# Hand-ordered queues of a two-model forward pass: SSD slots, a gated-conv branch and the opening in another order

## The chip, the cores and the metric

The kernel runs on one core of a Trainium2 chip. The metric is device time in microseconds (us), lower is better. Before the change it is 1112.82 us, the median of 3 runs (1112.5 to 1112.93).

## What is computed

Two models in a row on 256 tokens of width 1024 (272 with 16 meta tokens in the first). The first has an SSD (state space) mixer, a squared-ReLU MLP, a latent-attention mixer and another MLP; the second has a block with neighbourhood attention and a short gated convolution side by side, and an MLP. Cut to the parts that the change touches:

```python
# SSD mixer (8 groups of 4 heads, state 128, chunk 128)
z, xbc, dt = split(h @ w_in)
xbc = silu(causal_depthwise_conv(xbc, conv_w, conv_b))        # width 4
xs, b_in, c_in = split(xbc)
dt = softplus(dt + dt_bias);  a = -exp(a_log)
a_cs = cumsum(dt * a)
y = sum over s <= l of (C_l . B_s) * exp(a_cs[l] - a_cs[s]) * dt_s * x_s   # + d_skip * xs
g = y * silu(z);  g = g * rsqrt(mean(g * g, group) + eps) * norm_g;  out = g @ w_out

# second model's block
q, k, v, cb, cc, ch, ga, gb = split(rms_norm(x) @ w_in)
y_a = neighbourhood_attention(q, k, v, rpb) @ w_attn_branch
y_b = (cb * conv3(cc * ch)) @ w_conv_branch
x = x + (sigmoid(ga) * y_a + sigmoid(gb) * y_b) @ w_o
```

## The kernel before

Activations lie with features on the 128 partitions and tokens in the free dimension. Every fp32 product is made of three fp32r matmuls: weight and input are each split in a rounded part (`w_hi`, `x_hi`) and the rest (`w_lo`, `x_lo`), and PE adds hi*hi, hi*lo and lo*hi (`tile`, L450 ff). Weights stream as pages of 128x1024: SP loads a page into one of four slots `w_raw`, ACT rounds it (`hi`, L942), DVE or POOL subtracts (`lo`, L1423 on DVE, L2060 on POOL), PE uses it. A pair of pages is a chunk; `lin_chunk(c, k, n)` (L467) first waits until the PSUM buffer of its parity has been drained (`free`), then runs the two pages into `lin`.

There is no scheduler. Each engine's program is written out by hand, and the order of its lines is the order of its queue; semaphores join the queues.

**Opening** (L491 ff on PE, L974 ff on ACT, L1459 ff on DVE). The first norm's squares are summed by eight matmuls on ones; two of the squares are made on DVE (`square_raw`), six on ACT (`square_h` and L992). Meanwhile dt and the first group's x are projected from the unnormalised input. DVE scales dt, adds the bias (L1489), makes its modulus (L1491, L1493), ACT takes exp and ln of it, and DVE makes softplus, the product with a and the running sum `acs` (L1497 to L1502), before it drains the first x (`first_xs`, L1508). POOL writes `acs` to DRAM and reads it back, broadcast over the partitions (`acs_rows`), for the decays that ACT makes (`decay_logs`, `decay`).

**SSD slots** (`slot` on each engine). Slot s makes three projections for group s (x; B and C; z), the scan of group g = s-1, and the group norm of gs = s-2. PE: first projection, `cb_products`, `x_transposes`, second projection, `group_stat` (ones times `y_sum`), third projection, `y_products`. ACT: two decays, the z sigmoid (exp, ln, exp), page c+2.0, `conv0` (the convolution's first tap), page c+2.1, the square of y2, decay logs, the x sigmoid, and so on. DVE: `w_lo` of page c+2.0, `causal_cb`, the three other taps (`conv`, L1533), the clamp before the sigmoid, `scaled_tokens`, `head_mix`. POOL: the acs rows, y2, y_sum, then the `w_lo` of three pages. Slots 0 and 1 are written out, 2 to 7 in loops, 8 and 9 without projections.

**Second block** (`for i in range(20)` on PE, ACT and DVE). Iteration i projects chunk i, which DVE drains. Beside it runs the attention: head n has its maxima, exp and weighting (`weigh2`) in iteration n+6 of ACT and DVE; PE transposes its probabilities into ps7 at the top of iteration n+8 (L890), and DVE copies ps7 to `p_t2` in its iteration n+7, behind its second page. `values2(j)` (L901) multiplies heads 2j and 2j+1, behind the projection in PE's iteration 2j+9. `yb` = cb * conv is made on DVE at the end of iterations 10 and 11, rounded on ACT (`yb_hi`), and its rest `yb_lo` follows at once on DVE.

```python
    pe.wait_ge(pt2_done, 2 * j + 2)            # values2(j)
```

## Time and profile before

| | before |
|---|---|
| median of 3 runs | 1112.82 us |
| profiled execution, its own time | 1112.04 us |
| its span | 1110.4 us |
| granted PE clock | 1.00 of full speed |
| PE, weight loads busy | 1096.2 us (99%), 1067.3 us (96%) |
| DVE, ACT, POOL busy | 766.8 us (69%), 653.5 us (59%), 165.0 us (15%) |
| DMA | 171 GB/s mean |

The span runs from the first to the last instruction. A busy PE is one that has a matmul in flight; an idle stretch is named after the instruction that ended it. DVE is VectorE, ACT is ScalarE, POOL is GpSimd. In the slots DVE and ACT are busy for over nine tenths of the time, elsewhere for about half.

### The profile page before, as it was taken

What the parts mean: (1) busy time and instruction counts of PE and PEld (TensorE: products, weight loads), DVE (VectorE), ACT (ScalarE), POOL (GpSimd) and SP (SyncE); (2) the same over time, 40 slices, a digit from 0 to 9 for tenths busy, and PEclk for the clock granted to TensorE, in tenths of its full rate; (3) what the DMA queues carried; (4) which work ended last, traced back from release to release, by engine and by line L of the source; (5) the groups of instructions that cost most, each with busy time, mean ns of one, the idle gap of its engine ahead of it and who ended that gap; (6) DMA issues with size and microseconds to landing.
All of it is one profiled execution on the core that took longest, in us unless ns stands there. A gap on an engine that the chain in (4) does not pass through costs nothing.

```text
span 1110.4 us, 24004 instructions
## 1 busy us (share of the span) xinstructions
PE 1096.2 (99%) x8963; PEld 1067.3 (96%) x8963; DVE 766.8 (69%) x1154; ACT 653.5 (59%) x1075; POOL 165.0 (15%) x152
## 2 busy tenths in 40 slices
PE   9999999999999999999999999999999999999998
PEld 8999999999999999988899999999998999999998
DVE  7988999778565555588686665558787687666543
ACT  7899999655554433577565554446546655555331
POOL 0435434317000000112020000000003201000000
PEclk9999999999999999999999999999999999999999
DMA  6544544585545454443265555555444555555552
GB/s 240 205 157 156 185 153 159 151 260 167 174 171 179 163 187 171 134 136 113 73 213 188 182 187 181 181 195 172 152 151 144 182 181 187 183 189 188 182 182 91
DMA packets 53226, 189.96 MB, mean 171 GB/s; under 512 B 5920, under 2 KB 7200, under 8 KB 53168
## 3 DMA queue, kind: packets, MB, share of 16 engines
q1 hardware_dynamic: 51408, 182.59, 48.5%
...
q8 instruction: 38, 0.62, 0.2%
...
HBM read 188.07 MB, written 1.08 MB: 170 GB/s over the span
## 4 chain that ended last, share of the span: by engine, by line
PE 70%; DVE 14%; ACT 9%; issue 4%; DMA 2%; ACTq 0%; POOL 0%; DVEq 0%; SPq 0%
PE lin L462 22%; PE lin L464 22%; PE lin L463 22%; DVE w_lo L1426 4%; ACT w_hi L947 3%; DMA w_raw<-w 2%; DVE cv L1533 1%; ACT cv L1038 1%; ACT ee L1062 1%; DVE sg L1543 1%; ACT sg L1021 1%; ACT dd L1052 1%; DVE s_m L1836 1%; ACT sg L1019 1%; ACT pr L1347 1%
## 5 line engine op out<-in xcount | busy, mean ns | idle before, releaser
L1426 DVE TENSOR_TENSOR w_lo<-w_raw,w_hi 128x1024 fp32r<-128x1024 f32 (+3 forms) x318 | 382.2, 1204 | 252.6 <-ACT w_hi L947 251.9
L947 ACT ACTIVATE w_hi<-w_raw 128x1024 fp32r<-128x1024 f32 (+2 forms) x342 | 351.9, 1034 | 225.6 <-PE lin L464 212.9
L462 PE MATMUL lin<-x_hi,w_hi 128*128 128x256 f32 (+1 forms) x1504 | 432.3, 287 | 3.0 <-DVE cv L1533 2.4
L464 PE MATMUL lin<-x_hi,w_lo 128*128 128x256 f32 (+1 forms) x1504 | 428.4, 285 | 0.0
L463 PE MATMUL lin<-x_lo,w_hi 128*128 128x256 f32 (+1 forms) x1504 | 427.4, 284 | 0.0
L462 PEld LDWEIGHTS lin<-x_hi,w_hi 128*128 128x128 f32 x1504 | 283.6, 189 | 5.9 <-issue 3.6
L464 PEld LDWEIGHTS lin<-x_hi,w_lo 128*128 128x128 f32 x1504 | 283.8, 189 | 0.0
L463 PEld LDWEIGHTS lin<-x_lo,w_hi 128*128 128x128 f32 x1504 | 283.0, 188 | 0.5
L464 PE MATMUL lin<-hid_hi,w_lo 128*128 128x256 f32 (+1 forms) x768 | 218.2, 284 | 0.0
L463 PE MATMUL lin<-hid_lo,w_hi 128*128 128x256 f32 (+1 forms) x768 | 217.9, 284 | 0.0
L462 PE MATMUL lin<-hid_hi,w_hi 128*128 128x256 f32 (+1 forms) x768 | 217.4, 283 | 0.0
L464 PEld LDWEIGHTS lin<-hid_hi,w_lo 128*128 128x128 f32 x768 | 145.1, 189 | 0.0
L462 PEld LDWEIGHTS lin<-hid_hi,w_hi 128*128 128x128 f32 x768 | 145.0, 189 | 0.0
L463 PEld LDWEIGHTS lin<-hid_lo,w_hi 128*128 128x128 f32 x768 | 144.3, 188 | 0.0
L2058 POOL TENSOR_TENSOR h_sq<-h_sq 128x256 f32<-128x256 f32 (+1 forms) x35 | 30.3, 865 | 448.5 <-ACT h_sq L960 447.1
L1167 ACT ACTIVATE relu<-lin 128x512 f32<-128x512 f32 (+1 forms) x48 | 29.1, 606 | 82.6 <-PE lin L464 82.6
L2063 POOL TENSOR_TENSOR w_lo<-w_raw,w_hi 128x1024 fp32r<-128x1024 f32 x24 | 58.7, 2447 | 74.2 <-ACT w_hi L947 74.2
L956 ACT ACTIVATE x_hi<-h,vecs 128x256 fp32r<-128x256 f32 (+2 forms) x40 | 20.3, 508 | 42.1 <-DVE h L1708 37.7
L462 PE MATMUL lin<-g_hi,w_hi 128*128 128x272 f32 x144 | 42.2, 293 | 0.8 <-issue 0.4
L1691 DVE TENSOR_TENSOR hid_lo<-relu_sq,hid_hi 128x512 f32 (+1 forms) x48 | 34.4, 717 | 11.2 <-DVE relu_sq L1687 11.2
L464 PE MATMUL lin<-g_hi,w_lo 128*128 128x272 f32 x144 | 41.7, 289 | 0.0
L463 PE MATMUL lin<-g_lo,w_hi 128*128 128x272 f32 x144 | 41.5, 288 | 0.0
...
## 6 DMA issues: line engine op xcount, KB each, us to landing
...
```

What stands on the lines that cost most here:

```text
L462: mm3(o, wh, xh, start=first and i == 0, stop=False)
L463: mm3(o, wh, xl, start=False, stop=False)
L464: ins = mm3(o, wl, xh, start=False, stop=last and i == kts - 1)
L947: a(w_hi[pg.slot][:, 0:n], w_raw[pg.slot][:, 0:n], ACT.Copy).then_inc(w_hi_done, pages)
L956: a(x_hi[:, kt.value, 0:width(norm)], h[:, kt.value, tokens(norm)], ACT.Copy, scale=gain(norm, kt.value)).then_inc(xh_done, 1)
L1019: a(buf, buf if x is None else x, ACT.Exp, scale=-1.0).then_inc(step_sem, 1)
L1021: a(buf, buf, ACT.Ln, bias=1.0).then_inc(step_sem, 1)
L1167: a(relu[i][:, :, 0:n], linp(k, slice(0, n)), ACT.Relu).then_inc(drained[k.parity], 1)
L1426: tt(w_lo[pg.slot][:, 0:n], w_raw[pg.slot][:, 0:n], w_hi[pg.slot][:, 0:n].bitcast(F32), ALU.subtract)\
L1691: tt(hid_lo[:, bass.ds(at.value, 2), 0:n], relu_sq[i][:, :, 0:n], hid_hi[:, bass.ds(at.value, 2), 0:n].bitcast(F32), ALU.subtract).then_in ...
L2058: tt(h_sq[:, 0, 0:n], h_sq[:, 0, 0:n], h_sq[:, kt, 0:n], ALU.add).then_inc(hsum_done, 1)
L2063: tt(w_lo[pg.slot][:, 0:n], w_raw[pg.slot][:, 0:n], w_hi[pg.slot][:, 0:n].bitcast(F32), ALU.subtract)\
```

## The change

It adds and removes no matmul and no page. What moves:

- Opening: squares 6 and 7 go from ACT to DVE, before its last two `raw_lo`. The dt bias and the modulus are done by ACT (Abs and Relu with a bias) instead of three DVE instructions, and the three sums of dt come on DVE after `first_xs` and another page. On POOL two `w_lo` stand ahead of the wait for the acs write.
- Slots: on ACT `conv0` and both pages stand ahead of the z sigmoid; on DVE `w_lo` of page c+2.0 comes after the convolution; on POOL the first `w_lo` comes before y_sum, and the acs rows for the next slot are fetched before the last `w_lo` of this one; on PE the group statistic moves into the middle of the third projection.
- Second block: the copy to `p_t2` moves from behind the second page of DVE's iteration n+7 to the top of n+8; `yb` from the end of 10 and 11 to the top of 11 and 12; `yb_hi` and `yb_lo` to 11 and 12.

```diff
@@ -493,7 +493,7 @@
             for kt, (squared, count) in enumerate(((hsq_done, 1), (hsq_done, 2), (hsq_dve, 1), (hsq_dve, 2),
-                                                   (hsq_done, 3), (hsq_done, 4), (hsq_done, 5), (hsq_done, 8))):
+                                                   (hsq_done, 3), (hsq_done, 8), (hsq_dve, 3), (hsq_dve, 4))):
@@ -510,7 +510,7 @@
-                pe.wait_ge(dt_dve, 5)
+                pe.wait_ge(dt_dve, 3)
@@ -577,10 +577,11 @@
                 if has_lin:
                     lin_chunk(c + 1, k + 1, T, 0 if first else None)
-                if has_stat:
-                    group_stat(s + (-2))
-                if has_lin:
-                    lin_chunk(c + 2, k + 2, T)
+                    free(k + 2)
+                    for j in range(2):
+                        tile(lin[:, 2 * (k + 2).parity + j, 0:T], (c + 2).page(j), x_hi, x_lo, T).then_inc(w_used, 1)
+                        if has_stat and j == 0:
+                            group_stat(s + (-2))
@@ -984,12 +985,10 @@
             square_h(0, At(4))
-            square_h(0, At(5))
+            a(h_sq[:, 5, :], h[:, 5, :], ACT.Square).then_inc(hsq_done, 5)
             round_raw(6)
             round_raw(7)
             hi(Page(0), DT_PAGE, pages=2)
-            square_h(0, At(6))
-            a(h_sq[:, 7, :], h[:, 7, :], ACT.Square).then_inc(hsq_done, 3)
             hi(Page(2))
             norm_inv(0)
             hi(Page(3))
@@ -1002,10 +1001,14 @@
             hi(At(2).page(0))
+            dt_bias = v(V_DTB, rows=slice(0, 32))
+            act.wait_ge(drained[0], 1)
+            a(dta[:, :], dtb[:, :], ACT.Abs, bias=dt_bias).then_inc(dt_act, 1)
             round_hn(4)
-            act.wait_ge(dt_dve, 2)
+            act.wait_ge(dt_act, 2)
             a(dta[:, :], dta[:, :], ACT.Exp, scale=-1.0).then_inc(dt_act, 1)
-            act.wait_ge(dt_act, 2)
+            a(dtx[:, :], dtb[:, :], ACT.Relu, bias=dt_bias).then_inc(dt_act, 1)
+            act.wait_ge(dt_act, 3)
             a(dta[:, :], dta[:, :], ACT.Ln, bias=1.0).then_inc(dt_act, 1)
             round_hn(5)
@@ -1067,13 +1070,14 @@
                     decay(g, 0)
                     decay(g, 1)
+                if has_lin:
+                    conv0(s, 0)
+                    hi((c + 2).page(0))
+                    hi((c + 2).page(1))
+                if has_scan:
                     kz = g.times(3, K_GRP + 2)
                     act.wait_ge(drained[kz.parity], kz.half + 1)
                     sigmoid(z_sg[:, :, :], zg_step, g.times(3), z_raw[:, :, :])
-                if has_lin:
-                    hi((c + 2).page(0))
-                    conv0(s, 0)
-                    hi((c + 2).page(1))
                 if has_stat:
                     act.wait_ge(y2_done, (gs + 1).value)
                     a(h_sq[:, 0:2, :], y2[:, :, :], ACT.Square).then_inc(ysq_done, 1)
@@ -1392,8 +1396,8 @@
                     exps2(i - 6)
-                if i in (10, 11):
-                    j = i - 10
+                if i in (11, 12):
+                    j = i - 11
                     act.wait_ge(yb_done, j + 1)
                     a(yb_hi[:, 2 * j:2 * j + 2, :], yb[:, 2 * j:2 * j + 2, :], ACT.Copy).then_inc(ybh_done, 1)
@@ -1467,8 +1471,12 @@
-            for kt in range(2, KD):
+            for kt in range(2, 6):
                 raw_lo(kt)
+            square_raw(6)
+            square_raw(7)
+            raw_lo(6)
+            raw_lo(7)
             lo(Page(0), DT_PAGE)
             dve.sem_inc(w_lo_done[1], 1)
             lo(Page(2))
@@ -1484,30 +1492,22 @@
                 if kt == 1:
                     dve.wait_ge(w_used, 1)
                     tt(dtb[:, :], lin[r32, 0, 0:T], r_inv[r32, :], ALU.mult).then_inc(drained[0], 1)
-                if kt == 2:
-                    dve.wait_ge(drained[0], 1)
-                    ts(dtb[:, :], dtb[:, :], v(V_DTB, rows=r32), None, ALU.add).then_inc(first_bias, 1)
...
-                    tt(dta[:, :], dtb[:, :], dtx[:, :], ALU.max).then_inc(dt_dve, 1)
                 if kt in (3, 5):
                     lo(At(2).page(kt // 2 - 1))
-            dve.wait_ge(dt_act, 3)
-            stt(dt_t[:, :], dtb[:, :], 0.0, dta[:, :], ALU.max, ALU.add).then_inc(dt_dve, 1)
...
-            nc.vector.tensor_tensor_scan(acs[:, :], cst[r32, N_ONES:N_ONES + 1].broadcast_to([32, T]), dtx[:, :],
             lo(At(3).page(0))
...
             lo(At(3).page(1))
+            dve.wait_ge(dt_act, 5)
+            tt(dt_t[:, :], dtx[:, :], dta[:, :], ALU.add).then_inc(dt_dve, 1)
+            dve.wait_ge(dt_dve, 1)
+            ts(dtx[:, :], dt_t[:, :], a_exp[:, 0:1], -1.0, ALU.mult, ALU.mult).then_inc(dt_dve, 1)
...
+            nc.vector.tensor_tensor_scan(acs[:, :], cst[r32, N_ONES:N_ONES + 1].broadcast_to([32, T]), dtx[:, :],
@@ -1616,10 +1616,10 @@
                 if has_lin:
-                    lo((c + 2).page(0))
                     if has_scan:
                         causal_cb(g)
                     conv(s, 0)
+                    lo((c + 2).page(0))
                     clamp(sg[:, 0:2, :], cv[:, 0:2, :]).then_inc(clamped, 1)
@@ -1934,6 +1934,17 @@
             for i in range(20):
                 c, k = At(C_IN2 + i), At(K_IN2 + i)
+                if 8 <= i < 16:
+                    dve.wait_ge(pT2_done, i - 7)
...
+                    nc.vector.tensor_copy(p_t2[i % 2][:, :], ps7[:, :]).then_inc(pt2_done, 1)
+                if i in (11, 12):
+                    j = i - 11
+                    dve.wait_ge(drained[(k + (-1)).parity], (k + (-1)).half + 1)
...
+                    tt(yb[:, 2 * j:2 * j + 2, :], cv2[:, 2 * j:2 * j + 2, :], cb_r[:, 2 * j:2 * j + 2, :], ALU.mult)\
+                        .then_inc(yb_done, 1)
                 lo((c + 2).page(0))
                 dve.wait_ge(w_used, (c + 1).page().value)
@@ -1950,11 +1961,6 @@
                 lo((c + 2).page(1))
-                if 7 <= i < 15:
-                    dve.wait_ge(pT2_done, i - 6)
...
-                    nc.vector.tensor_copy(p_t2[(i + 1) % 2][:, :], ps7[:, :]).then_inc(pt2_done, 1)
@@ -1999,12 +2005,8 @@
                 if 6 <= i < 14:
                     weigh2(i - 6)
-                if i in (10, 11):
-                    j = i - 10
...
-                    tt(yb[:, 2 * j:2 * j + 2, :], cv2[:, 2 * j:2 * j + 2, :], cb_r[:, 2 * j:2 * j + 2, :], ALU.mult)\
-                        .then_inc(yb_done, 1)
+                if i in (11, 12):
+                    j = i - 11
                     dve.wait_ge(ybh_done, j + 1)
@@ -2070,10 +2072,8 @@
-            def slot(s, has_lin=True, has_stat=True):
+            def slot(s, has_lin=True, has_stat=True, has_rows=True):
                 c, gs = s.times(3, C_GRP), s + (-2)
-                if has_lin and s.base:
-                    acs_rows(s)
                 if has_stat:
...
                     tt(y2[:, :, :], y1[:, :, :], z_s[gs.parity][:, :, :], ALU.mult).then_inc(y2_done, 1)
+                if has_lin:
+                    lo((c + 2).page(1))
+                if has_stat:
                     pool.wait_ge(ysq_done, (gs + 1).value)
                     tt(y_sum[:, :], h_sq[:, 0, :], h_sq[:, 1, :], ALU.add).then_inc(ysum_done, 1)
                 if has_lin:
-
-                    lo((c + 2).page(1))
                     lo((c + 3).page(1))
+                    if has_rows:
+                        acs_rows(s + 1)
                     lo((c + 4).page(1))
 
-            pool.wait_ge(dt_dve, 5)
+            pool.wait_ge(dt_dve, 3)
             pool.dma_start(acs_dram, acs[:, :]).then_inc(acs_out, 16)
+            lo(At(C_GRP + 3).page(0))
+            lo(At(C_GRP + 3).page(1))
             pool.wait_ge(acs_out, 16)
             acs_rows(At(0))
-            lo(At(C_GRP + 3).page(0))
-            lo(At(C_GRP + 3).page(1))
             lo(At(C_GRP + 4).page(1))
+            acs_rows(At(1))
             slot(At(1), has_stat=False)
             with pool.Fori(0, 2) as turn:
                 for i in range(2):
                     slot(At(2 + i, 2, turn))
             slot(At(6))
-            slot(At(7))
+            slot(At(7), has_rows=False)
             slot(At(8), has_lin=False)
             slot(At(9), has_lin=False)
```

How the queues stand. First ACT in the loop over the SSD slots, just after the two decays (ee): before,

```order
L1062 ACTIVATE ee<-dd 128x864
L1071 ISA
L1019 ACTIVATE z_sg<-z_raw 128x544
L1020 ISA
L1021 ACTIVATE z_sg<-z_sg 128x544
L1022 REGISTER_ALU
L1023 ACTIVATE z_sg<-z_sg 128x544
L944 ISA
L946 ISA
L947 ACTIVATE w_hi<-w_raw 128x1024
L1032 REGISTER_ALU
```

and in the change (cv is conv0):

```order
L1065 ACTIVATE ee<-dd 128x864
L1035 ISA
L1041 ISA
L1041 REGISTER_ALU
L1041 ACTIVATE cv<-lin,vecs 128x272
L1041 ISA
L1041 ACTIVATE cv<-lin,vecs 128x272
L945 ISA
L947 REGISTER_ALU
L948 ACTIVATE w_hi<-w_raw 128x1024 x2
L1079 REGISTER_ALU
L1022 ACTIVATE z_sg<-z_raw 128x544
```

The two instructions of conv0 and the two pages now stand between the decays and the z sigmoid. Second, POOL in the same loop, one turn of the change:

```order
L2083 TENSOR_TENSOR y<-y,z_s 128x544
L2064 ISA
L2065 TENSOR_TENSOR w_lo<-w_raw,w_hi 128x1024
L2088 TENSOR_TENSOR y_sum<-h_sq 128x272
L2064 REGISTER_ALU
L2065 TENSOR_TENSOR w_lo<-w_raw,w_hi 128x1024
L2071 REGISTER_ALU
L2073 ISA
L2073 DMA acs_bc<-acs_dram 128x1088
L2064 REGISTER_ALU
L2065 TENSOR_TENSOR w_lo<-w_raw,w_hi 128x1024
```

Before, the DMA stood ahead of the product y2 (written y here), y_sum right behind it, and the three w_lo in a row at the end. Third, DVE from the weighting of head 4 (pr) to the next maxima in the second block: before,

```order
L1932 TENSOR_SCALAR pr<-pr,rinv 128x256 x2
L2006 TENSOR_TENSOR cv<-cv,cb_r 128x512
L2010 TENSOR_TENSOR yb_lo<-cv,yb_hi 128x512
L1426 TENSOR_TENSOR w_lo<-w_raw,w_hi 128x1024
L1951 TENSOR_TENSOR cb_r<-lin,r_inv 128x512
L1426 TENSOR_TENSOR w_lo<-w_raw,w_hi 128x1024
L1957 COPY p_t<-ps 128x512
L1987 TENSOR_TENSOR ya_lo<-ps,ya_hi 128x256
```

and in the change:

```order
L1932 TENSOR_SCALAR pr<-pr,rinv 128x256 x2
L1941 COPY p_t<-ps 128x512
L1946 TENSOR_TENSOR cv<-cv,cb_r 128x512
L1430 TENSOR_TENSOR w_lo<-w_raw,w_hi 128x1024
L1962 TENSOR_TENSOR cb_r<-lin,r_inv 128x512
L1430 TENSOR_TENSOR w_lo<-w_raw,w_hi 128x1024
L1993 TENSOR_TENSOR ya_lo<-ps,ya_hi 128x256
```

cv<-cv,cb_r is yb. Its rest, yb_lo, no longer follows it but comes behind the next weighting; the copy of ps7 has changed places with a page, a drain and a page.

## Rows read from the trace of the kernel before

**Rows 1.** What TensorE (PE) waited for, whole span: waiting line <- releaser: total us, times, longest.
```profile
PE ps L890 <- DVE pr L1932: 2.9, 3, 1.3
PE lin L462 <- DVE cv L1533: 2.4, 5, 0.8
...
PE ps L540 <- DVE bc_s L1547: 0.4, 1, 0.4
...
PE lin L462 <- issue: 0.4, 1, 0.4
PE ps L548 <- POOL y_sum L2085: 0.3, 1, 0.3
...
PE lin L462 <- DVE g_lo L1577: 0.3, 1, 0.3
```
**Rows 2.** Timeline of PE in SSD slots: start us, duration us, instruction, count [idle before].
```profile
55.52 0.24 PE L567 MATMUL ps<-mm,x_tok 128*64 128x16 f32 x4
55.69 0.39 PE L462 MATMUL lin<-x_hi,w_hi 128*128 128x272 f32 x1
...
130.42 0.62 PE L540 MATMUL ps<-bc_s 128*128 128x272 f32 x2
...
138.12 0.62 PE L548 MATMUL ps<-y_sum,cst 128*128 128x272 f32 x2
...
146.30 0.24 PE L567 MATMUL ps<-mm,x_tok 128*64 128x16 f32 x4
146.93 0.39 PE L462 MATMUL lin<-x_hi,w_hi 128*128 128x272 f32 x1 [0.39 <-DVE cv L1533]
```
**Rows 3.** Timeline of ScalarE (ACT) in the same slot.
```profile
130.76 0.64 ACT L1019 ACTIVATE z_sg<-z_raw 128x544 f32<-128x544 f32 x1
...
132.69 1.04 ACT L947 ACTIVATE w_hi<-w_raw 128x1024 fp32r<-128x1024 f32 x1
...
136.74 1.95 ACT L1052 ACTIVATE dd<-acs_bc,cols 128x272 f32<-128x272 f32 x6 [0.58 <-DMA acs_bc<-acs_dram]
139.69 0.66 ACT L1019 ACTIVATE sg<-sg 128x544 f32<-128x544 f32 x1 [1.00 <-DVE sg L1543]
```
**Rows 4.** Timeline of VectorE (DVE) in the same slot.
```profile
133.76 1.23 DVE L1426 TENSOR_TENSOR w_lo<-w_raw,w_hi 128x1024 fp32r<-128x1024 f32 x1 [1.67 <-ACT w_hi L947]
...
138.03 1.63 DVE L1543 TENSOR_SCALAR sg<-cv 128x544 f32<-128x544 f32 x1
...
144.28 2.51 DVE L1533 SCALAR_TENSOR_TENSOR cv<-lin,vecs,cv 128x271 f32<-128x271 f32 x6
146.90 0.45 DVE L1543 TENSOR_SCALAR sg<-cv 128x544 f32<-128x544 f32 x1
```
**Rows 5.** Timeline of GpSimd (POOL) in the same slot.
```profile
136.97 2.38 POOL L2063 TENSOR_TENSOR w_lo<-w_raw,w_hi 128x1024 fp32r<-128x1024 f32 x1
144.65 2.37 POOL L2063 TENSOR_TENSOR w_lo<-w_raw,w_hi 128x1024 fp32r<-128x1024 f32 x1 [5.29 <-ACT w_hi L947]
```
**Rows 6.** Timeline of PE in the opening, second projection.
```profile
22.08 0.29 PE L464 MATMUL lin<-x_hi,w_lo 128*128 128x272 f32 x1
22.49 0.39 PE L462 MATMUL lin<-x_hi,w_hi 128*128 128x272 f32 x1
```
**Rows 7.** Timeline of PE, then of DVE, in the second block's attention.
```profile
833.52 0.66 PE L890 MATMUL ps<-cst,pr 128*128 128x128 f32 x4 [1.08 <-DVE pr L1932]
...
839.80 1.08 PE L901 MATMUL ps<-p_t,v 128*64 128x256 f32 x8
842.20 0.66 PE L890 MATMUL ps<-cst,pr 128*128 128x128 f32 x4 [1.32 <-DVE pr L1932]
...
825.76 0.69 DVE L2010 TENSOR_TENSOR yb_lo<-cv,yb_hi 128x512 fp32r<-128x512 f32 x1 [0.70 <-ACT yb_hi L1398]
826.71 1.23 DVE L1426 TENSOR_TENSOR w_lo<-w_raw,w_hi 128x1024 fp32r<-128x1024 f32 x1 [0.26 <-ACT w_hi L947]
...
835.72 1.23 DVE L1426 TENSOR_TENSOR w_lo<-w_raw,w_hi 128x1024 fp32r<-128x1024 f32 x1 [0.26 <-ACT w_hi L947]
```

20 lines of the change are left out of this document (7 added, 13 removed).

## The prediction

> **What bounds the kernel now.** I read the page first: TensorE (PE) is busy in 99% of the span, at the full granted clock, and the other engines are well below it. So the time is the sum of the PE's matmuls plus the moments in which it waits, and an edit that adds or removes no matmul can only move those moments. The second view is the list of what PE waited for [rows 1]. All of it is small: the longest groups are 2.9 us before the transposes of the probabilities (L890) and 2.4 us before projections behind the convolution on VectorE (DVE, L1533). The third view is the timeline of each engine in one SSD slot [rows 2 to 5], the fourth the opening [rows 6], the fifth the second block's attention [rows 7]. Everything outside them (the MLPs, the MLA block) is untouched.
>
> **The SSD slots.** A slot on PE is: first projection, cb products and x transposes, second projection, group statistic, third projection, y products. After the last y matmul the next slot's projection starts 0.63 us later (146.30 to 146.93), where the trace also shows the same step without a wait: 0.17 us (55.52 to 55.69) [rows 2]. So a stalled slot loses 0.46 us, of which 0.39 is shown as idle. Rows 1 have five such waits with 2.4 us and one put down to issue with 0.4; with 0.07 of refill for each of the six that makes 3.2 us. That is the most the slots can give.
>
> Why is the convolution late? I follow it back. The slot's second convolution starts on DVE at 144.28, right behind work that runs without a gap from 133.76. There DVE had stood idle for 1.67 us until ScalarE (ACT) rounded the page w_hi [rows 4]. ACT came to that page at 132.69, because the z sigmoid (three instructions from 130.76, 1.93 us) stood ahead of it [rows 3]. In the same chain the clamp at 138.03 takes 1.63 us where its like at 146.90 takes 0.45: it lies under POOL's w_lo (from 136.97, 2.38 us long) and ends 0.3 us after it [rows 4, 5]. ACT then waits 1.00 us for that clamp, and before it 0.58 us for the DMA of acs rows [rows 3].
>
> The change puts conv0 and both w_hi pages ahead of the z sigmoid, takes w_lo page 0 behind the convolution on DVE, lets POOL do its w_lo before y_sum, and issues the acs DMA a slot part earlier. I count from E, the end of the first projection (130.42). Before, conv0 ran at E+3.2. Now ACT is free at E+0.3 (130.76), so conv0 ends at E+1.3, and the two pages at E+2.2 and E+3.2 (a page row is 1.04 long [rows 3], about 1 us each). POOL's w_lo follows: E+3.2 to E+5.6 (2.4). DVE has the cb products at about E+1.0, masks them (0.6), convolves (2.5) and is at w_lo page 0 at E+4.1; POOL holds it off until E+5.6, so it ends at E+6.8. The z sigmoid and the square (1.93+0.6) end on ACT at E+5.8; y_sum (0.8) then stands behind that w_lo, and the clamp behind y_sum: clamp done near E+8.0, against 139.66 = E+9.2 before. ACT and DVE gain about 1.2 us, more than the 0.46 that is missing. After six slots without the stall the chain still has about 0.8 us to spare, so I take the whole 3.2 us. Bounds: 0 (the chain finds another brake) and 3.2.
>
> Here the lock matters. In this trace an op of DVE that reads two SBUF tiles or clamps one ends 0.3 us behind POOL's w_lo, while the convolution, which reads PSUM and one SBUF tile, takes 2.51 us under POOL's w_lo of 144.65 as well [rows 4, 5]. The Trainium skill, SBUF — State Buffer, section Who interferes with whom, states it as an exclusive lock for whole instructions between GpSimd and DVE ops with two SBUF inputs or in a two-port mode; the rows agree with it. Without a lock page 0 would be ready at E+5.3 instead of E+6.8. PE wants it at 138.12 = E+7.7 [rows 2]: either way in time, so the sum stays, but by the lock only 0.9 us is left, and on that the slower rival below rests.
>
> The group statistic moves behind the third projection's first page. It costs what it costs now; PE does the same matmuls. Its cover only grows: y_sum is due 3 us later.
>
> **Behind the last slot** PE waits once for y_sum (0.3 us) and once for g_lo (0.3 us) [rows 1]. POOL and ACT come to y_sum 0.8 us earlier, so I take the first, with 0.2 of refill: 0.5 us. The g_lo chain hangs on the statistic itself; I take nothing for it, and 0.4 as the upper bound.
>
> **The opening.** Two squares leave ACT and are done by DVE before its last two raw_lo. ACT's next page is bound by its DMA there, so r_inv comes when it did; nothing gained, nothing lost. Three instructions on dt leave DVE's chain ahead of the w_lo and x_lo that PE waits for, and the dt sums go behind first_xs. PE's gap of 0.41 from 22.08 to 22.49, against a pace of 0.125, is such a wait: 0.28 us [rows 6]. The wait before the first cb products (0.4 in rows 1, 0.1 of refill) shrinks, since ACT gets to its sigmoids earlier. Together 0.8 us. What is made later: acs, by some 2 us, and the first acs rows behind two w_lo on POOL (2.4 each) [rows 5]. They are read on ACT some 10 us later, so I count nothing; if that cover is gone, ACT waits and the 0.8 is lost. Abs on ACT is not in this trace; the nearest row is the first step of the z sigmoid, 0.64 us on 128x544 [rows 3], and dt has 32x272, so with Relu it is 0 to 1.3 us of ACT time, of which most stands where ACT waited for DVE's modulus. I take nothing for it. The Trainium skill, ScalarE: Activation LUTs, section Table sets: the hidden batching unit, has abs and relu in every set, so by it no table is loaded for them; no row here shows Abs.
>
> **The second block.** PE waits for weigh2 (pr, L1932) three times, 2.9 us [rows 1]: 1.08 before 833.52, 1.32 before 842.20, just after the values of 839.80 [rows 7], and so 0.5 once more. DVE is late because iterations 10 and 11 carry yb: after yb it waits 0.70 us for ACT's yb_hi, and 0.26 us for the page behind that [rows 7]. In the change yb stands at the top of the next iteration and yb_lo at its end; ACT makes yb_hi while DVE scales pr, so both waits go: 0.96 us in each of two iterations, 1.9 us. And yb starts one iteration later, so the first late iteration is on time.
>
> But the copy of ps7 into p_t moves from the middle of an iteration to the top of the next, and PE's values2 need it. It has the shape of yb_lo, 0.69 us [rows 7]. Before, iteration 11 begins at 826.71 and 12 at 835.72 [rows 7], 9.0 us. In the change iteration 10 lacks yb, yb_lo and the waits (2 x 0.6 + 0.96), and since iteration 7 has no copy DVE comes about 0.8 us earlier all along: 11 begins at 823.7. It lasts 9.0-0.96 = 8.05, 12 (without the 0.35 of ya_lo) 7.7: iteration 13 begins at 839.4 and its copy ends at 840.0. PE, without its first wait, would be at these values at 839.80-1.08 = 838.7: a new wait of about 1.3 us. PE then starts the next transposes at 841.1, not 842.2, and the last wait (0.5, 0.2 of refill) is gone: gain 1.1+0.7 = 1.8 us. Bounds: 0, and 3.2 (2.9 and refill).
>
> **Sum.** 3.2+0.5+0.8+1.8 = 6.3 us. The profiled execution took 1112.04 us (span 1110.4 and 1.6 around it), so it would be 1105.7; the median of the runs, 1112.82, is 0.8 above it: **1106.5 us**.
>
> **Rivals.**
> - The second block gives nothing: values2 wait for the copy as long as the transposes did for pr. For it: the copy is due just as PE comes at every odd iteration. Against: DVE is freed of 1.9 us of waiting. 1108.3 us, chance 0.15.
> - The slots give half: ACT has only 1.58 us of idle time in a slot (0.58+1.00) and the slot shrinks by 0.46, so a new wait there leaves part of the stall. 1108.1 us, chance 0.12; with the one above, 1109.9.
> - Everything goes, the 3.2 of the second block and g_lo's wait too: 8.1 us, 1104.7 us, chance 0.05.
> - Slower: the third projection waits for w_lo page 0, in all six slots. It is ready at E+6.8, due at E+7.7; should ACT's second page, and POOL's w_lo and DVE's behind it, come over 0.9 us later than I count, each further microsecond costs six. At 2.4 us late it is 6 x 1.5 = 9 us: 1106.5+9 = 1115.5. It turns slower from 2.3 us late on. Against it: conv0 is tied to PE's own pace, and ACT has its idle time to catch up. Chance 0.05.
> - The change does not do what it says, since DVE and ACT drift to the same order of waits: 1112.8 us, chance 0.03.
>
> **Chances.** Forecast 0.60, rivals as above. A measurement of this kernel can tell about 0.2% (2.2 us) from no change, so faster means below 1110.6: the forecast and the first three rivals, 0.92, less 0.04 for mixtures that end near the bound: 0.88. Same 0.07, slower 0.05. The range: the low end is the full gain, 1104.5; the high end takes in most of the first two rivals together, 1109.6.
>
> **What would show it.** In the slots: no PE idle before the first projection; ACT's conv0 right behind decay; the DVE w_lo of page 0 longer than 1.2 us, ending 0.3 to 1.5 us behind POOL's; no idle before the dd rows; period of a slot near 22.2 us instead of 22.65. In the second block: one wait of PE before values2 near 840, of 1 to 1.5 us, and none for pr. In the opening: the gap near 22.3 gone, acs written about 2 us later. Wrong it is if PE shows waits for w_lo at the third projection, for acs DMA through ACT, or for p_t copies at each odd iteration.

## The result, and the profile after

The changed kernel takes 1104.33 us (median of 4 runs, 1103.82 to 1104.87) against 1112.66 us before in the same session: ratio 0.9925, 95% interval 0.9908 to 0.9942. That is 8.3 us less, where 6.3 were forecast, and 0.17 us below the low end of the range. Both profiled executions agree with it: 1112.04 us before, 1103.82 after (span 1102.1, clock 1.00), 8.2 less.

Medians of one kernel differ by 0.3 us between sessions (1112.66 to 1112.94 for the kernel before), so the parts are read from landmarks in PE's timeline. In kernels that share the code in question, the slots repeat within 0.3 us (150.29 to 150.55) and the second block within 0.1 (58.84 to 58.92). First what PE waits for after the change, the answer to [rows 1] (waiting line <- releaser: total us, times, longest):

```profile
PE ps L494 <- DVE mm L1447: 1.3, 1, 1.3
PE ps L902 <- DVE p_t L1941: 0.7, 1, 0.7
PE lin L737 <- POOL q_n L2160: 0.5, 1, 0.5
PE lin L462 <- DVE x_lo L1440: 0.4, 2, 0.2
PE ps L768 <- DVE o_lo L1858: 0.4, 1, 0.4
PE lin L505 <- DVE w_lo L1430: 0.3, 1, 0.3
PE ps L784 <- DVE p_t L1854: 0.3, 1, 0.3
```

Of the six groups of [rows 1] none is left, and PE's wait for the last squares of the first norm, 0.6 us before, is gone too. One wait has come in the second block (p_t, 0.7) and one in the opening (the w_lo of dt's page, 0.3, since two squares now stand ahead of it on DVE).

The landmarks, PE's timeline after (start us, duration, instruction, count): slot 2's first projection; in a slot the cb products, the third projection, the last y product and the next projection; y_sum and the output projection behind the last y products; the first transposes and the last values of the second block's attention.

```profile
149.31 0.62 PE L540 MATMUL ps<-bc_s 128*128 128x272 f32 x2
...
157.01 0.29 PE L462 MATMUL lin<-x_hi,w_hi 128*128 128x272 f32 x1
...
165.19 0.24 PE L567 MATMUL ps<-mm,x_tok 128*64 128x16 f32 x4
165.36 0.39 PE L462 MATMUL lin<-x_hi,w_hi 128*128 128x272 f32 x1
...
198.45 0.62 PE L548 MATMUL ps<-y_sum,cst 128*128 128x272 f32 x2
...
790.90 0.60 PE L891 MATMUL ps<-cst,pr 128*128 128x128 f32 x4
...
847.15 1.08 PE L902 MATMUL ps<-p_t,v 128*64 128x256 f32 x8
```

The projection at 165.36 follows the y products after 0.17 us, as the unstalled one of [rows 2], not after 0.63. No slot from 3 on has a wait before it. By these landmarks:

| from PE's timeline, us | before | after | gain | forecast |
|---|---|---|---|---|
| opening: start of slot 2's first projection | 55.69 | 54.07 | 1.6 | 0.8 |
| slots 2 to 7: from there to the next projection after slot 7 | 136.54 | 133.49 | 3.05 | 3.2 |
| slot 8: to the projection behind its y products | 13.75 | 13.19 | 0.6 | 0.5 |
| from there to the second block's first transposes | 590.47 | 590.15 | 0.3 | 0 |
| second block: to its last values2 | 58.92 | 56.25 | 2.7 | 1.8 |

The sum is 8.2 us, what the profiled executions differ by. The fourth row is the least certain: where POOL's slots are as before, this stretch takes 590.09 to 590.55 us (seven kernels), and 589.5 to 590.7 over all of the study, so its 0.3 can't be told from scatter. One slot of the change, on ACT, DVE and POOL (the slot whose E, the end of the first projection, is 149.31; compare [rows 3], [rows 4] and [rows 5], with E at 130.42):

```profile
149.72 1.05 ACT L1041 ACTIVATE cv<-lin,vecs 128x272 f32<-128x272 f32 x2 [0.95 <-PE lin L464]
150.66 2.00 ACT L948 ACTIVATE w_hi<-w_raw 128x1024 fp32r<-128x1024 f32 x2
152.56 0.65 ACT L1022 ACTIVATE z_sg<-z_raw 128x544 f32<-128x544 f32 x1
...
155.04 1.93 ACT L1055 ACTIVATE dd<-acs_bc,cols 128x272 f32<-128x272 f32 x6
157.21 0.66 ACT L1022 ACTIVATE sg<-sg 128x544 f32<-128x544 f32 x1 [0.24 <-DVE sg L1543]
...
150.95 2.51 DVE L1533 SCALAR_TENSOR_TENSOR cv<-lin,vecs,cv 128x271 f32<-128x271 f32 x6
153.58 2.66 DVE L1430 TENSOR_TENSOR w_lo<-w_raw,w_hi 128x1024 fp32r<-128x1024 f32 x1
156.16 1.01 DVE L1543 TENSOR_SCALAR sg<-cv 128x544 f32<-128x544 f32 x1
...
152.74 2.41 POOL L2065 TENSOR_TENSOR w_lo<-w_raw,w_hi 128x1024 fp32r<-128x1024 f32 x1 [1.49 <-ACT w_hi L948]
155.22 1.65 POOL L2088 TENSOR_TENSOR y_sum<-h_sq 128x272 f32<-128x272 f32 x1
```

Forecast and measured, counted from E: ACT's pages end at 3.2 and 3.35; POOL's w_lo 3.2 to 5.6 and 3.4 to 5.8; DVE's w_lo of page 0 ends at 6.8 and 6.9; the clamp is done at 8.0 and 7.9; the third projection comes at 7.7 and 7.7. The slot ran as it was written down.

### The profile page after: what moved, and what is told of

The parts are those of the page before. It is cut to its first block, busy times and chain, and to the rows that moved or that the text cites. A ratio compares the mean times of both kernels' runs of the same rounds, so it can differ in the third digit from the quotient of the medians.

```text
span 1102.1 us, 24005 instructions
## 1 busy us (share of the span) xinstructions
PE 1094.4 (99%) x8963; PEld 1066.9 (97%) x8963; DVE 771.8 (70%) x1153; ACT 653.9 (59%) x1075; POOL 170.6 (15%) x152
## 4 chain that ended last, share of the span: by engine, by line
PE 85%; DVE 10%; ACT 2%; issue 2%; DMA 1%; POOL 0%; SPq 0%; DVEq 0%; ACTq 0%
PE lin L462 27%; PE lin L464 26%; PE lin L463 26%; DVE w_lo L1430 3%; DMA w_raw<-w 1%; PE ps L561 1%; DVE s_m L1836 1%; DVE x_lo L1440 1%; DVE p_t L1854 1%; ACT w_hi L948 0%; ACT pr L1351 0%; DVE s_m L1918 0%; PE ps L540 0%; DVE p_t L1941 0%; DVE q_ss L1779 0%
## 5 line engine op out<-in xcount | busy, mean ns | idle before, releaser
L1430 DVE TENSOR_TENSOR w_lo<-w_raw,w_hi 128x1024 fp32r<-128x1024 f32 (+3 forms) x318 | 392.6, 1237 | 237.6 <-ACT w_hi L948 236.6
```

What stands on the lines that cost most here:

```text
L1430: tt(w_lo[pg.slot][:, 0:n], w_raw[pg.slot][:, 0:n], w_hi[pg.slot][:, 0:n].bitcast(F32), ALU.subtract)\
```

## The experiments

Fifteen further kernels, all read at the same landmarks. The table gives the start of ACT's r_inv, slot 2's first projection, the time from there to the projection behind slot 8's y products (the slots), the second block's stretch, and the median. How each was edited, and what it says, follows.

| kernel | r_inv | slot 2 | slots | block | median us |
|---|---|---|---|---|---|
| before | 11.54 | 55.69 | 150.29 | 58.92 | 1112.66 to 1112.94 |
| the change | 10.69 | 54.07 | 146.68 | 56.25 | 1104.33 |
| e1 opening alone | 10.74 | 53.94 | 150.54 | 58.91 | 1110.7 |
| e2 slots alone | 11.55 | 55.81 | 146.59 | 58.86 | 1108.55 |
| e3 second block alone | 11.39 | 56.12 | 150.44 | 56.26 | 1109.99 |
| e4 change, yb at 14 and 15 | 10.82 | 54.05 | 146.63 | 55.49 | 1103.0 |
| e5 before, squares moved | 11.02 | 55.46 | 150.55 | 58.84 | 1111.82 |
| e6 before, dt moved | 12.05 | 55.24 | 150.32 | 58.85 | 1111.38 |
| e7 change, z sigmoid ahead | 11.23 | 54.45 | 153.16 | 56.19 | 1110.56 |
| e8 change, DVE's w_lo ahead | 11.30 | 54.54 | 146.56 | 56.21 | 1103.96 |
| e9 change, y_sum ahead | 11.34 | 54.57 | 150.69 | 56.30 | 1108.89 |
| e10 change, copy back | 11.52 | 54.76 | 146.59 | 56.51 | 1104.6 |
| e11 before, ACT's order alone | 11.57 | 55.94 | 151.30 | 58.87 | 1112.99 |
| e12 before, yb at 14 and 15 | 11.34 | 55.77 | 150.42 | 55.49 | 1109.41 |
| e13 before, ACT's and POOL's order | 11.30 | 55.63 | 147.19 | 58.86 | 1108.86 |
| e14 change, acs rows back | 10.72 | 53.93 | 146.85 | 56.24 | 1105.32 |
| e15 change, statistic ahead | 10.76 | 54.02 | 147.46 | 56.29 | 1104.56 |

### The three parts by themselves (e1, e2, e3)

Each takes one part of the diff above into the kernel before and leaves the rest: e1 the hunks at 493, 510, 984, 1002, 1467 and 1484 with the two `w_lo` ahead of POOL's wait for the acs write, e2 those at 577, 1067 and 1616 with the rest of POOL's, e3 those at 1392, 1934, 1950 and 1999. Of e1, e2 and e3 two lines each, in that order:

```diff
+            square_raw(6)
+            square_raw(7)
...
-                    lo((c + 2).page(0))
...
+                    lo((c + 2).page(0))
...
+                if 8 <= i < 16:
...
-                if 7 <= i < 15:
```

> The kernel before with the opening of the change alone (squares 6 and 7 on DVE, dt's bias and modulus on ACT, dt's sums behind first_xs, POOL's two w_lo ahead of the wait for the acs write); slots and second block as before. Theory (the three parts add up, and the opening gave 1.6 us, not 0.8): slot 2's first projection starts 1.6 us earlier than in the kernel before, the start of the output projection also 1.6, total 1.6 us less. Rival 1 (half of the 1.6 was a DMA that happened to land early in the profiled run of the change): 0.8 us at slot 2 and in the total. Rival 2 (without the slot's new order the earlier opening is eaten by the slots' stalls, since ACT and DVE set their pace): 1.6 at slot 2, but under 0.5 at the output projection.

> The kernel before with the slots of the change alone (ACT, DVE, POOL and PE orders); opening and second block as before. Theory: the six stalls before the first projection go and the tail's waits too: the output projection starts 3.0 us earlier counted from slot 2, the MLP 3.9 us, total 3.9 us less. Rival (the slots need the head start that the opening gives): the stall stays in the first two or three slots, 2 us or less.

> The kernel before with the second block's edit alone (copy to p_t2 at the top of the next iteration, yb one iteration later). Theory: the waits of the transposes for pr go and one wait of 0.7 to 0.8 us before values2 takes their place, 2.7 us less. Rival (what is gained there depends on what comes before): 1.8 us or less. By the sum of the parts 1.6 + 3.9 + 2.7 = 8.2 us, against 8.3 measured.

Medians 2.24, 4.39 and 2.95 us below the kernel before (1112.94 there; ratios 0.998 [0.9971, 0.999], 0.9961 [0.9946, 0.9975], 0.9974 [0.9965, 0.9984]). By the landmarks: 1.75 at slot 2 for e1, 3.70 in the slots for e2, 2.66 in the second block for e3. By the landmarks each part is as large alone as in the change, so they do not help or hinder each other. The three medians add up to 9.6 us, about 1 us more than the change's 8.3, which no landmark explains. All rivals here are out, the one on the DMA only partly: see e5.

### The opening (e5, e6)

e5 takes the squares' part into the kernel before (ACT without squares 6 and 7, DVE with them, PE's order), e6 the rest of the opening: dt's bias and modulus on ACT, the sums behind `first_xs`, POOL's two w_lo ahead of its wait. The lines that tell them apart, e5 first:

```diff
-            square_h(0, At(6))
-            a(h_sq[:, 7, :], h[:, 7, :], ACT.Square).then_inc(hsq_done, 3)
```

```diff
+            a(dta[:, :], dtb[:, :], ACT.Abs, bias=dt_bias).then_inc(dt_act, 1)
...
-            stt(dt_t[:, :], dtb[:, :], 0.0, dta[:, :], ALU.max, ALU.add).then_inc(dt_dve, 1)
```

> The kernel before with only the two squares moved from ScalarE to VectorE in the opening. Theory A (the step of the prediction that failed is that ScalarE's page of 9.97 was not bound by its DMA but stood behind the squares, which run to 10.06 without idle time): r_inv starts near 10.7 instead of 11.54, slot 2 begins 0.8 to 1.0 us earlier. Rival B (as predicted: the page waits for its DMA): r_inv within 0.2 us of where it was, and nothing gained at slot 2.

> The kernel before with only dt's bias and modulus on ScalarE, dt's sums behind first_xs, and the two w_lo of GpSimd ahead of its wait. Theory A: r_inv as before, slot 2 begins 0.7 to 0.8 us earlier, the size that was predicted for the whole opening. Rival B (the 1.6 us of the opening all come from the dt instructions): 1.6 us at slot 2. Rival C (the dt part gains only behind an earlier r_inv): under 0.3.

In the profiled executions neither has what was expected in full: slot 2 starts 0.23 us earlier in e5, 0.45 in e6, and 1.6 to 1.75 where both are in. But one pair is a weak measure here: the five other kernels with the old opening start slot 2 at 55.63 to 56.12. The medians say more. e5 lies 0.95 us and e6 1.39 us below the kernel before (1112.77 in their session, 10 runs of each against 25), together 2.3 us, as e1's 2.24. So the two parts add up, and the squares are worth about what theory A said, though the interval of e5 does not exclude nothing (ratios 0.9993 [0.9983, 1.0002] and 0.9987 [0.9977, 0.9997]). What one execution can lose is seen in ACT's timeline. First the kernel before, with PE's wait for the squares, then the change, then e5:

```profile
PE ps L498 <- ACT h_sq L960: 0.6, 1, 0.6
```

```profile
9.65 0.41 ACT L992 ACTIVATE h_sq<-h 128x272 f32<-128x272 f32 x1
9.97 1.04 ACT L947 ACTIVATE w_hi<-w_raw 128x1024 fp32r<-128x1024 f32 x1
```

```profile
8.93 1.36 ACT L948 ACTIVATE w_hi<-w_raw 128x256 fp32r<-128x256 f32 x2
10.19 0.47 ACT L971 ACTIVATE r_ln<-ps,eps_t 128x272 f32<-128x272 f32 x1
10.69 0.43 ACT L973 ACTIVATE r_inv<-r_ln 128x272 f32<-128x272 f32 x1
```

```profile
9.55 1.06 ACT L947 ACTIVATE w_hi<-w_raw 128x1024 fp32r<-128x1024 f32 x1 [0.33 <-DMA w_raw<-w]
...
11.02 0.43 ACT L972 ACTIVATE r_inv<-r_ln 128x272 f32<-128x272 f32 x1
```

Before, the page follows the last square with no idle time: it was not waiting for its DMA. The six other kernels with ACT's squares in place (e2, e3, e6, e11, e12, e13) show the same. In the change r_inv starts 0.85 us earlier. In e5 the same page waits 0.33 us for its DMA, and r_inv is 0.52 earlier. The other kernels with the new opening split into two kinds: r_inv at 10.69 to 10.82 in the change, e1, e4, e14 and e15, and 11.23 to 11.52 in e7 to e10, where ACT waits for a DMA (0.80 us for this page in e10, 0.64 in e8, or for `h` earlier in e7 and e9). In e10 r_inv comes at 11.52, as it did before. So the arrival of the first transfers scatters by 0.8 us, and that is what the squares' move can lose. The late ones (e5 and e7 to e10) were all measured on one chip, e1, e4, e14 and e15 on two others; whether the scatter belongs to the execution or to the chip is not shown.

What is left when r_inv is taken out is regular: from r_inv to slot 2 it is 43.2 to 43.4 us wherever dt has moved (e6 too, whose inputs landed 0.5 us later) and 44.1 to 44.7 wherever it has not. The dt part is thus worth 0.8 us between the two profiled executions (44.15 and 43.38), as was forecast for the whole opening, and 1.1 between the medians of all. With dt in its old place PE waits before the first cb products, 0.4 us before and 0.6 in e5; e2, e3 and e11 to e13 have 0.5 to 1.0 with the squares unmoved, so e5's 0.6 is no effect of the squares. With dt moved the wait is 0.2 (e6) or absent (e1, the change and all kernels made from it). PE's gap of 0.41 near 22.3 [rows 6] is gone in the change as well.

### The slots: which of the moves counts

e7, e8, e9, e14 and e15 start from the change, e11 and e13 from the kernel before. e7:

```diff
+                if has_scan:
+                    sigmoid(z_sg[:, :, :], zg_step, g.times(3), z_raw[:, :, :])
                 if has_lin:
                     conv0(s, 0)
                     hi((c + 2).page(0))
                     hi((c + 2).page(1))
-                if has_scan:
-                    sigmoid(z_sg[:, :, :], zg_step, g.times(3), z_raw[:, :, :])
```

> The kernel of the change with ScalarE's z sigmoid again ahead of the slot's first convolution and the two pages; all else as in the change. This is the slower rival of the prediction, made on purpose. Theory: everything behind it is 1.93 us later; GpSimd's w_lo runs from E+5.3 to E+7.7 (E is the end of the first projection), VectorE's w_lo of page 0 is held off by it and ends near E+8.9, and the third projection is due at E+7.7: 1.2 us of waiting and 0.1 to 0.2 of refill in each of slots 1 to 7, 8 to 10 us more than the change. Rival 1 (VectorE is not held off): its w_lo ends at E+7.1, no wait there, and only a part of the old stall of 0.46 per slot comes back, under 3 us. Rival 2 (the queues catch up over the slots): waits only in every second slot, 4 to 5 us.

e7 is 6.2 us slower than the change (medians) and 6.5 in the slots: 1.75 in slot 2, 0.85 to 0.97 in each of slots 3 to 7, 0.24 in slot 8. This is the slower rival of the prediction, and it is real. DVE and POOL of e7, then PE (E is 154.12):

```profile
159.51 3.06 DVE L1430 TENSOR_TENSOR w_lo<-w_raw,w_hi 128x1024 fp32r<-128x1024 f32 x1
```

```profile
159.08 2.41 POOL L2065 TENSOR_TENSOR w_lo<-w_raw,w_hi 128x1024 fp32r<-128x1024 f32 x1 [2.35 <-ACT w_hi L948]
```

```profile
162.72 0.36 PE L462 MATMUL lin<-x_hi,w_hi 128*128 128x272 f32 x1 [0.73 <-DVE w_lo L1430]
```

POOL holds the w_lo off until 161.49, it ends at E+8.45, and PE stands idle for 0.73 us, in all slots together 4.8 us in six waits (the first is 1.6). The expectation was 8 to 10 us: it counted E+8.9, since it took 0.3 us for ACT's way to the z sigmoid, which here starts at E.

e8:

```diff
                 if has_lin:
+                    lo((c + 2).page(0))
                     if has_scan:
                         causal_cb(g)
                     conv(s, 0)
-                    lo((c + 2).page(0))
```

> The kernel of the change with VectorE's w_lo of page 0 again ahead of the mask of the cb products and the convolution in the slots; all else as in the change. Theory (the z sigmoid's move alone takes the stall away; w_lo's place does not matter once its page comes 2 us earlier): w_lo at E+2.3 to E+3.5, convolution to E+6.7, the clamp done near E+7.2 instead of E+7.9; no wait of TensorE in the slots, total within 0.5 us of the change. Rival (the new place is needed, since the convolution comes 1.2 us later and with it all behind it): TensorE waits again before the next slot's first projection, 1 to 3 us slower.

146.56 us in the slots against 146.68: the new place of DVE's w_lo gives nothing.

e11 is the kernel before with ACT's edit alone:

```diff
+                if has_lin:
+                    conv0(s, 0)
+                    hi((c + 2).page(0))
+                    hi((c + 2).page(1))
                 if has_scan:
...
                     sigmoid(z_sg[:, :, :], zg_step, g.times(3), z_raw[:, :, :])
-                if has_lin:
-                    hi((c + 2).page(0))
-                    conv0(s, 0)
-                    hi((c + 2).page(1))
```

> The kernel before with one edit alone: in the slots ScalarE's first convolution and two pages ahead of the z sigmoid. VectorE, GpSimd, TensorE, the opening and the second block as before. Theory (this move alone takes the stall away): the slots from slot 2 on last 22.20 us, the output projection starts 3.0 us earlier, total 3 us less, and 0.3 to 0.9 of the tail on top or not. Rival 1 (the DMA of the acs rows, which comes 0.58 us late for ScalarE, and VectorE's clamp under GpSimd's w_lo keep half of it): 22.4 us per slot, 1.5 us. Rival 2 (all four parts are needed): under 0.5 us, or slower, since y_sum comes later than the group statistic that stands ahead of the third projection.

Nothing gained: ratio 1.0001 [0.9991, 1.001]. The slots are even 1.0 us longer, most of it in slots 2 and 3 (23.7 and 23.1 us, against 23.2 and 22.7). Rival 2 allowed for slower, but by a late y_sum, and PE waits for y_sum no more than before (0.3 us, once). In slot 2 ACT waits 2.35 us for the acs rows, where the kernel before has 1.02:

```profile
70.95 1.95 ACT L1052 ACTIVATE dd<-acs_bc,cols 128x272 f32<-128x272 f32 x6 [2.35 <-DMA acs_bc<-acs_dram]
```

They landed 6.7 us after their issue there, 5.3 before; whether the order or scatter did that, and what lengthens slot 3, is open. So moving the z sigmoid, to which the prediction gave the stall, is not enough. e9 is the change with POOL's y_sum back ahead of its first w_lo:

```diff
-                if has_lin:
-                    lo((c + 2).page(1))
                 if has_stat:
                     pool.wait_ge(ysq_done, (gs + 1).value)
                     tt(y_sum[:, :], h_sq[:, 0, :], h_sq[:, 1, :], ALU.add).then_inc(ysum_done, 1)
                 if has_lin:
+                    lo((c + 2).page(1))
                     lo((c + 3).page(1))
```

> The kernel of the change with GpSimd's y_sum again ahead of its first w_lo in the slots; all else as in the change. Theory (the z sigmoid's move alone takes the stall away): y_sum ends near E+6.6 and the w_lo of page 1 at E+9.0, due at E+11; VectorE's w_lo of page 0 is not held off and ends near E+5.4. No wait of TensorE in the slots, total within 0.5 us of the change. Rival (GpSimd's order is needed): that w_lo holds off VectorE's product of ee and cbm (at E+8.8 in the change) or is late for the third projection; 1 to 5 us slower.

4.6 us slower than the change, 4.0 of them in the slots: the rival, not the theory. What happens is nearly the same in both. In e11 (E is 154.26) POOL's w_lo waits behind y_sum, y_sum for the square, and that for the z sigmoid wherever it stands; then it lies on DVE's clamp:

```profile
160.17 0.77 POOL L2086 TENSOR_TENSOR y_sum<-h_sq 128x272 f32<-128x272 f32 x1 [2.57 <-ACT h_sq L1080]
160.90 2.37 POOL L2064 TENSOR_TENSOR w_lo<-w_raw,w_hi 128x1024 fp32r<-128x1024 f32 x1
```

```profile
161.73 1.85 DVE L1544 TENSOR_SCALAR sg<-cv 128x544 f32<-128x544 f32 x1
```

The clamp is done at E+9.3, no earlier than in the kernel before (E+9.2). In e9 the largest stalls, 1.2 us of PE's time each, are those behind slots 4 and 7. There too the w_lo lies on the clamp, for longer, since DVE's w_lo of page 0 now stands right ahead of the clamp and holds POOL's up first (slot 4, POOL, DVE and PE):

```profile
112.14 3.38 POOL L2065 TENSOR_TENSOR w_lo<-w_raw,w_hi 128x1024 fp32r<-128x1024 f32 x1
```

```profile
113.18 2.63 DVE L1543 TENSOR_SCALAR sg<-cv 128x544 f32<-128x544 f32 x1
```

```profile
123.08 0.38 PE L462 MATMUL lin<-x_hi,w_hi 128*128 128x272 f32 x1 [1.19 <-DVE cv L1533]
```

In slot 6 of e9 (E is 151.44), with a stall of 0.3, it lies on the product of ee and cbm instead, which takes 3.25 us, not 2.0:

```profile
159.03 2.62 POOL L2065 TENSOR_TENSOR w_lo<-w_raw,w_hi 128x1024 fp32r<-128x1024 f32 x1
```

```profile
160.28 3.25 DVE L1571 TENSOR_TENSOR mm<-ee,cbm 128x864 f32<-128x864 f32 x2
```

From these two comes the theory that both orders are needed, and only they. e13 is e11 with POOL's w_lo ahead of y_sum, nothing else:

```diff
+                if has_lin:
+                    lo((c + 2).page(1))
+                if has_stat:
                     pool.wait_ge(ysq_done, (gs + 1).value)
                     tt(y_sum[:, :], h_sq[:, 0, :], h_sq[:, 1, :], ALU.add).then_inc(ysum_done, 1)
                 if has_lin:
-
-                    lo((c + 2).page(1))
```

> The kernel before with two edits: in the slots ScalarE's first convolution and two pages ahead of the z sigmoid, and GpSimd's w_lo of page c+2.1 ahead of y_sum. VectorE, TensorE, the place of the acs rows, the opening and the second block as before. Theory (the stall is GpSimd's w_lo, which stands behind y_sum and holds off VectorE's clamp; it needs its page early and its place in the queue, both): GpSimd's w_lo runs from E+3.4 to E+5.8, over VectorE's convolution, the clamp is done near E+7.2 against E+9.2 before; 22.20 us per slot, no wait before the first projections, 3.0 us less at the output projection, 3 to 3.9 us in all. Rival (a third piece is needed): 22.4 us or more per slot, 1.5 us or less.

From slot 3 on every slot lasts 22.20 us. The slots give 3.1 us and the stretch behind them 0.9, of which 0.3 is g_lo's wait, now gone, and the rest within that stretch's scatter. 1108.86 us in all is 3.9 less than before (ratio 0.9966 [0.9952, 0.998]). DVE's clamp and POOL's w_lo in e13 (E is 151.38):

```profile
155.53 2.50 DVE L1534 SCALAR_TENSOR_TENSOR cv<-lin,vecs,cv 128x271 f32<-128x271 f32 x6
158.07 0.44 DVE L1544 TENSOR_SCALAR sg<-cv 128x544 f32<-128x544 f32 x1
```

```profile
154.81 2.49 POOL L2064 TENSOR_TENSOR w_lo<-w_raw,w_hi 128x1024 fp32r<-128x1024 f32 x1 [1.44 <-ACT w_hi L947]
157.28 0.78 POOL L2089 TENSOR_TENSOR y_sum<-h_sq 128x272 f32<-128x272 f32 x1
```

POOL's w_lo now runs beside the convolution, which reads PSUM and is not held off (2.50 us, as in [rows 4]). The clamp takes 0.44 us and is done at E+7.1, as expected. That is the mechanism of the slots' 3 us, and these two orders are enough for it.

That both are needed is shown for POOL's alone (e9, e11). For ACT's it is not: in e7 DVE's w_lo stands behind the convolution, and it is this w_lo that PE waits for. No kernel has POOL's new order with ACT's and DVE's old ones. In the slot of [rows 3] to [rows 5] the page of POOL's w_lo is rounded by 135.6, just as DVE's convolution begins:

```profile
134.56 1.05 ACT L947 ACTIVATE w_hi<-w_raw 128x1024 fp32r<-128x1024 f32 x1
```

```profile
135.49 2.51 DVE L1533 SCALAR_TENSOR_TENSOR cv<-lin,vecs,cv 128x271 f32<-128x271 f32 x6
```

An estimate from these rows: POOL's w_lo, ahead of y_sum, would run from 135.6 to 138.0, and the clamp would be done between E+8.1 and E+8.7 (if y_sum holds it up), 0.5 to 1.1 us earlier than it was, where 0.46 is missing. y_sum would end near 138.8, too late for the statistic at 138.12, but not for its new place a page later. So POOL's order with PE's, and ACT untouched, is a rival that was not tested.

e14 puts the DMA of the acs rows back to the top of POOL's slot, e15 the group statistic back ahead of the third projection (e14's lines, then e15's):

```diff
+                if has_lin and s.base:
+                    acs_rows(s)
...
-                    if has_rows:
-                        acs_rows(s + 1)
```

```diff
-                    free(k + 2)
-                    for j in range(2):
-                        tile(lin[:, 2 * (k + 2).parity + j, 0:T], (c + 2).page(j), x_hi, x_lo, T).then_inc(w_used, 1)
-                        if has_stat and j == 0:
-                            group_stat(s + (-2))
+                if has_stat:
+                    group_stat(s + (-2))
+                if has_lin:
+                    lin_chunk(c + 2, k + 2, T)
```

> The kernel of the change with the DMA of the acs rows again at the top of GpSimd's slot. Theory (0.58 us of waiting on ScalarE, which is hidden there): ScalarE waits about 0.6 us before dd and is done with it near E+8.2, as the clamp is; no wait of TensorE, total within 0.5 us of the change. Rival (it is needed): the stall comes back in part, 1 to 3 us slower.

> The kernel of the change with TensorE's group statistic again ahead of the third projection. In the change y_sum ends at E+7.56 and the third projection begins at E+7.70. Theory: the statistic there is just in time or 0.1 to 0.3 us late in each of six slots: 0 to 2 us slower than the change. Rival (the statistic needs its new place, since y_sum stands behind a w_lo that may come later in some slots): more than 2 us slower.

In the slots of e14's profiled execution (1103.78 us) the acs rows matter by 0.2 us, one wait of PE in slot 2, within the 0.5 of the theory. The other of its two runs took 1106.86, 3 us more, and has no trace, so the median, 1.0 above the change's, decides nothing. ACT waits for the rows 1.37, 0.84 and 0.53 us in slots 2 to 4, and not at all from slot 5 on, where POOL is early enough:

```profile
67.94 1.95 ACT L1055 ACTIVATE dd<-acs_bc,cols 128x272 f32<-128x272 f32 x6 [1.37 <-DMA acs_bc<-acs_dram]
```

The statistic ahead costs 0.8 us: 0.6 in slot 2 and about 0.1 in every second slot. In slot 2 of e15 PE waits for y_sum:

```profile
68.61 0.72 PE L548 MATMUL ps<-y_sum,cst 128*128 128x272 f32 x2 [0.30 <-POOL y_sum L2087]
```

e13 has the same wait and 0.5 us more in the slots than the change. So the statistic's new place is the third piece, and a small one.

### The second block: the copy or yb (e4, e10, e12)

e4 is the change with yb later, e12 the kernel before with yb later (ACT's yb_hi and DVE's yb and yb_lo alike, 10 and 11 there), e10 the change with the copy to p_t2 where it was. e4, then e10:

```diff
-                if i in (11, 12):
-                    j = i - 11
+                if i in (14, 15):
+                    j = i - 14
```

```diff
-                if 8 <= i < 16:
-                    dve.wait_ge(pT2_done, i - 7)
...
                 lo((c + 2).page(1))
+                if 7 <= i < 15:
+                    dve.wait_ge(pT2_done, i - 6)
```

> The kernel of the change with yb, yb_hi and yb_lo in iterations 14 and 15 of the second block, behind the last weighting, rather than 11 and 12. Theory (the 0.66 us wait before values2 is DVE's lateness from yb and yb_lo, 1.3 us of DVE's time in each of two iterations, so the copy to p_t2 is late by their time): the wait goes, 0.8 us less than the change. Rival 1 (the copy is late because it stands at the top of the iteration, behind the weighting, with yb or without): the wait stays, no difference. Rival 2: the gate or the branch pages wait for DVE in iterations 14 to 16 instead; no difference or slower by up to 1 us.

> The kernel of the change with the copy to p_t2 at its old place, behind the second page of the iteration before; yb stays at 11 and 12. Theory A (the copy's new place causes the 0.66 us wait before values2, yb does not): no wait before values2, and none for pr, 0.8 us less than the change. Theory B (yb's 1.3 us per iteration are the load, and the copy only decides where they show): the 0.66 us before values2 go, but the transposes wait for pr of iteration 12 by 0.5 to 1 us and perhaps once more; within 0.5 us of the change, or up to 0.7 slower.

> The kernel before with one edit alone: yb, yb_hi and yb_lo in iterations 14 and 15 of the second block instead of 10 and 11; the copy to p_t2 at its old place. Theory (the load of yb in VectorE's iterations 10 and 11 is the whole cause of the waits for pr): all three waits go and no wait before values2 comes, 3.3 to 3.5 us less than before, more than the second block's part of the change (2.66). Rival (without the copy's new place the transposes still wait for pr): 2.0 us or less.

Both e4 and e12 take 55.49 us for the stretch, 0.76 less than the change and 3.43 less than before, with no wait for pr or p_t left. e10, where the copy stands in its old place, moves the loss to the transposes and keeps it (theory B of e10):

```profile
841.80 0.66 PE L891 MATMUL ps<-cst,pr 128*128 128x128 f32 x4 [0.79 <-DVE pr L1932]
```

So yb's load in DVE's busy iterations is the whole cause; the copy's new place is worth 0.3 us with yb at 11 and 12 and nothing with yb later. One edit of two numbers (e12) gains more in this block than the change's three. e4 is the fastest kernel of the study, 1103.0 us (1102.67 to 1103.03), ratio to the kernel before 0.991 [0.9893, 0.9927]. The change's own interval overlaps with it; that e4 is faster rests on the landmarks and on four runs of each that do not overlap.

## Where the prediction was right, and where it failed

The sum was 6.3 us and the two profiled executions differ by 8.2. Most of the missing 1.9 us is in two terms: the opening, 0.8 forecast and 1.6 measured, where a step was wrong, and the second block, 1.8 and 2.7, where a size was. The other terms came within about 0.3 us.

- **Bound by PE, waits only.** Right. PE's 8963 matmuls are the same in all kernels of the study, and each gain is that of waits which are gone from its list.
- **Slots, 3.2 us.** 3.05 measured, and all four times from E held within 0.2 us. The reason was at best half of it. The step "ACT came to that page at 132.69, because the z sigmoid (three instructions from 130.76, 1.93 us) stood ahead of it" gives the stall to ACT's order, which alone gives nothing (e11), because POOL's w_lo stays behind y_sum and on the clamp. With POOL's order it gives the whole (e13). The prediction had both in its chain, but called the sigmoid the cause; whether ACT's order is needed at all stays open.
- **The lock.** The trace after and e7, e9, e11 show it: a DVE instruction that reads two SBUF tiles, or clamps one, ends a little less than its own length behind POOL's instruction (clamp 0.3, w_lo 1.1 us behind; [rows 4] has only the clamp), and the convolution beside POOL's w_lo keeps its 2.50 us. The Trainium skill, SBUF — State Buffer, section Who interferes with whom, states an exclusive lock held for a whole instruction, which a DVE instruction with at most one SBUF input does not need outside the two-port modes; the traces agree.
- **Slower rival.** Its mechanism and its price are shown by e7: a delay of 1.93 us where 0.9 is free costs 6 x 1.03 = 6.2 us by the prediction's rule, and 6.5 were measured, though not evenly: 1.75 in slot 2 and 0.9 in each later one. In the change the slack is 0.8 us (E+6.9 against E+7.7), 0.9 forecast.
- **Tail, 0.5 us.** 0.6 for y_sum's wait. The 0.3 of g_lo, given only as a bound, is gone from the list too, though the stretch that it stands in scatters by more.
- **Opening, 0.8 us: the step that failed.** "ACT's next page is bound by its DMA there, so r_inv comes when it did" was wrong: in the profile of before the page has no idle time ahead of it, so it was bound by the squares in front of it. Taking them away brought r_inv 0.85 us forward in this execution. In others the DMA takes part of it back (e5, e7 to e9) or all (e10). The other 0.8 of the 1.6, the dt instructions, came as forecast: PE's gap near 22.3 and its wait before the first cb products are gone.
- **Abs and Relu at no cost.** Right: 0.51 us each on 32x272, with no load of a table beside them and no new wait of PE. By the Trainium skill, ScalarE: Activation LUTs, section Table sets: the hidden batching unit, abs and relu are in every set, so none was due; the trace agrees.
- **Second block, 1.8 us: mis-sized.** The waits for pr went, one wait before values2 came, at the place that was named. It measured 0.66 us, not 1.3. DVE's lead into iteration 11 was 0.6 us larger than the sum had it (it starts at 817.54, which is 823.1 on the clock of the kernel before, and 823.7 were written), and iterations 11 and 12 lasted 7.87 and 7.54 us, not 8.05 and 7.7. PE came to the values as forecast. The term was two large times subtracted, and its error was as large as the result.
- **The range.** The low end, 1104.5, held the full gain of slots and second block (8.1 us with g_lo's wait, 1104.7) but no gain for r_inv, which was counted at exactly nothing though the step behind it had no row.
